# A causal mask that is filled in, rotary queries computed turned, and heads and sample batches in a new order

## The reference

```python
q = (rmsnorm(q_lat, q_norm) @ w_uq).reshape(B, T, H_B, NOPE + ROPE)       # 8 heads, 128 + 64
q = concat([q[..., :NOPE], rope(q[..., NOPE:], pos)])
# rope: x1, x2 = halves of 32; [x1*cos - x2*sin, x2*cos + x1*sin]
s = einsum('bqhd,bshd->bhqs', q, k) * scale
s = where(k_chunk <= q_chunk, s, -inf)    # chunks of 64: masked per 64 x 64 block
o = einsum('bhqs,bshd->bqhd', softmax(s), v) * silu(gate)
x = x + rmsnorm(o @ w_out, norm_post)
```

## Time and profile before

| | us |
|---|---|
| three runs | 620.49, 621.52, 622.27 (median 621.52) |
| the profiled execution | 620.64 |
| its span, first to last instruction | 618.9 |
| TensorE busy | 599.2 (97%) |
| VectorE busy | 369.4 (60%) |
| ScalarE busy | 308.1 (50%) |
| GpSimd busy | 109.8 (18%) |

### The profile page before, as it was taken

How to read it: one execution, slowest core, us unless ns; L and a number is a source line. 1 busy time by engine, 2 the same in 40 slices (tenths; PEclk the granted TensorE clock), 3 DMA queues, 4 the chain that set the end, 5 groups by cost and what they waited for, 6 DMA issues and landing times.

```text
span 618.9 us, 11804 instructions
## 1 busy us (share of the span) xinstructions
PE 599.2 (97%) x4546; PEld 576.6 (93%) x4546; DVE 369.4 (60%) x574; ACT 308.1 (50%) x616; POOL 109.8 (18%) x173
## 2 busy tenths in 40 slices
PE   8999999999999999999999999999999988799996
PEld 7999999999999999999999999989998977699996
DVE  5485667464554872277536478467788875663415
ACT  6796463442362562267326324345656567662311
POOL 0100010010030143156407200110000033400002
PEclk9999999999999999999999999999999999999999
DMA  8932362271262273242425222231110155856004
GB/s 299 348 97 87 101 204 78 73 216 54 78 203 70 79 271 104 61 147 87 135 51 156 69 69 61 60 90 31 35 53 18 51 172 203 252 176 238 1 2 170
DMA packets 65431, 73.46 MB, mean 119 GB/s; under 512 B 8160, under 2 KB 57568, under 8 KB 65248
## 3 DMA queue, kind: packets, MB, share of 16 engines
q1 hardware_dynamic: 65376, 72.71, 36.8%
HBM read 61.92 MB, written 10.78 MB: 117 GB/s over the span
## 4 chain that ended last, share of the span: by engine, by line
PE 70%; DVE 12%; ACT 10%; issue 3%; DMA 3%; POOL 2%; SPq 1%; DVEq 0%; ACTq 0%; POOLq 0%
PE bank L1598 22%; PE bank L1600 21%; PE bank L1599 21%; DVE pT_lo L1297 2%; DMA x_nat<-in_x_sample_dram 2%; ACT prob L1239 2%; DVE sT_lo L1297 1%; ACT slab_hi L1033 1%; DVE slab_lo L1297 1%; PE bank L1874 1%; ACT sT_hi L1033 1%; PE bank L1645 1%; DVE rows L1293 1%; DMA x_raw<-in_xT_dram 1%; ACT qS L1033 1%
## 5 line engine op out<-in xcount | busy, mean ns | idle before, releaser
L1598 PE MATMUL bank<-slab_hi,hat_hi 128*128 128x256 f32 (+2 forms) x560 | 160.4, 286 | 1.8 <-DVE hat_lo L1297 1.0
L1600 PE MATMUL bank<-slab_hi,hat_lo 128*128 128x256 f32 (+2 forms) x560 | 159.3, 285 | 0.0
L1599 PE MATMUL bank<-slab_lo,hat_hi 128*128 128x256 f32 (+2 forms) x560 | 159.3, 285 | 0.0
L1598 PEld LDWEIGHTS bank<-slab_hi,hat_hi 128*128 128x128 f32 x560 | 105.3, 188 | 3.3 <-DVE slab_lo L1297 1.4
L1600 PEld LDWEIGHTS bank<-slab_hi,hat_lo 128*128 128x128 f32 x560 | 105.6, 189 | 0.6
L1599 PEld LDWEIGHTS bank<-slab_lo,hat_hi 128*128 128x128 f32 x560 | 105.2, 188 | 0.6
L1297 DVE TENSOR_TENSOR slab_lo<-stage,slab_hi 128x1024 fp32r<-128x1024 f32 (+3 forms) x70 | 83.7, 1196 | 26.7 <-ACT slab_hi L1033 25.5
L1598 PE MATMUL bank<-hat_hi,slab_hi 128*128 128x320 f32 x256 | 79.4, 310 | 0.7 <-DVE krL L1297 0.4
L1599 PE MATMUL bank<-hat_lo,slab_hi 128*128 128x320 f32 x256 | 78.7, 308 | 0.0
L1600 PE MATMUL bank<-hat_hi,slab_lo 128*128 128x320 f32 x256 | 78.7, 308 | 0.0
L1033 ACT ACTIVATE slab_hi<-stage 128x1024 fp32r<-128x1024 f32 (+3 forms) x70 | 71.0, 1014 | 6.1 <-DMA stage<-in_a_w_in_dram 1.5
(11 more groups left out here) (324 smaller groups left out, 1369.7 us busy)
## 6 DMA issues: line engine op xcount, KB each, us to landing
stage<-in_a_w_in_dram SPq DMA_DIRECT2D x22, 512.0 KB, 4.6
st_s<-in_state_gla_dram SPq DMA_DIRECT2D x4, 1024.0 KB, 6.7
out_dram<-st_s SPq DMA_DIRECT2D x4, 1024.0 KB, 5.1
stage<-in_a_w_out_dram SPq DMA_DIRECT2D x8, 512.0 KB, 4.3
stage<-in_b_w_in_dram SPq DMA_DIRECT2D x8, 512.0 KB, 4.5
stage<-in_ckvT_dram SPq DMA_DIRECT2D x8, 512.0 KB, 4.0
stage<-in_cache_ckv_dram SPq DMA_DIRECT2D x8, 512.0 KB, 6.5
stage<-in_b_w_out_dram SPq DMA_DIRECT2D x8, 512.0 KB, 4.2
```

The source lines that it names most:

```text
L1598: pe.matmul(out, a[0], b[0], start=first, stop=False)
L1599: pe.matmul(out, a[0], b[1], start=False, stop=False)
L1600: return pe.matmul(out, a[1], b[0], start=False, stop=last)
```

## The change

- The mask matmuls and their two constants go. In `S`, VectorE first writes -2^120 with one memset (64 partitions, two pieces of 64 columns) into the scores' bank in PSUM, waits for it, and then takes the maxima.
- The prompt's rotary queries are computed turned: weights (reordered on the host) are stationary, 512 tokens stream. `qr` (g, e) gives half e of four heads, 4 x 32 rows. VectorE rotates with tables laid out alike (`cosT`, `sinT`, loaded by SP in `ldt`); `qh` splits into high and low, and SP sets each head's 32 rows in `qS` with 16 DMAs of 64 KB per group of four heads, 32 in all. The samples' tile keeps the old way (`qo`, `qoT`), ahead of and behind a gate product.
- The rotary weights are loaded with two DMAs, not six.
- Order of heads: the `qabs` of a head comes right behind its scores, the last value tile behind the first head's key, the piece for head h + 4 is multiplied and copied right behind the turn, its low part (`plo`) last in the head; the cached batches are split likewise into `ct` (ScalarE) and `cl` (VectorE) and lie in heads 4 and 5, not 3 and 4.
- Order of sample batches: `ot` and `cr` ahead of `ct`, `cl` behind the scores' maxima, weight pieces at the end of a batch.
- In phase A's tail `xT` of tile 2 is ahead of `rs` of the last tile.

```diff
+        if NT <= t < NT + 3:
+            out += [("xT", "B", t - 3)]
         if t == NT:
             out += [("rs", NT - 1)]
-        if NT <= t < NT + 3:
-            out += [("xT", "B", t - 3)]
         if 0 <= t - 1 < NT - 1:
             out += [("rs", t - 1)]
...
-    out += [("gb", 2, 0), ("cT", 4)] + [("qT", t) for t in range(NT)] + [("gb", 2, 1)]
-    out += [("qr", 0)]
+    out += [("gb", 2, 0), ("cT", 4)] + [("qT", t) for t in range(NT)] + [("ldt",), ("gb", 2, 1)]
+    out += [("qr", 0, 0)]
     load(("gb", 1))
-    out += [("qr", 1), ("qr", 2), ("qrT", 0), ("gb", 1, 0), ("qrT", 1), ("qr", 3), ("qrT", 2), ("qr", 4)]
+    out += [("qr", 0, 1), ("qo",), ("gb", 1, 0), ("qh", 0), ("qoT",), ("qr", 1, 0)]
     load(("gb", 0))
-    out += [("gb", 1, 1), ("qrT", 3)]
+    out += [("qr", 1, 1), ("gb", 1, 1)]
     load(("uvn", 0))
     load(("uvn", 1))
-    out += [("gb", 0, 0), ("qrT", 4), ("gb", 0, 1)]
+    out += [("qh", 1), ("gb", 0, 0), ("gb", 0, 1)]
...
-    out += [("qn", 0), ("kh", 0), ("vh", 1, 2), ("vh", 1, 3), ("qabs", 0)]
-    load(("hd", 3))
+    out += [("qn", 0), ("kh", 0), ("vh", 1, 2)]
...
     for h in range(-1, HB):
         if h >= 0:
             out += [("T", h, 0), ("T", h, 1)]
-        if h == HB - 1:
-            out += [("Oh", h - 1), ("zr", 1), ("ct", 2), ("ss", 1)]
-        else:
-            out += [("S", h + 1, 0), ("S", h + 1, 1), ("N", h + 1, 0), ("N", h + 1, 1)]
+        if 0 <= h < 4:
+            out += [("piece", ("hd", h + 4), 0)]
+        elif 4 <= h < 6:
+            out += [("ct", h - 4)]
+        if h + 1 < HB:
...
-        if h == 6:
-            out += [("cr", 2), ("ot", 2), ("ss", 0)]
-        if h >= 0:
...
-        if h == 0:
-            out[out.index(("T", 0, 1)) + 1:out.index(("T", 0, 1)) + 1] = [("qabs", 1)]
-        if 0 <= h < 4:
...
+        if h == -1:
+            out += [("vh", 1, 3)]
+            load(("hd", 3))
         elif h == 5:
             out += [("zr", 0), ("cr", 0), ("ot", 0), ("cr", 1), ("ot", 1)]
+        elif h == 6:
+            out += [("cr", 2), ("ss", 0)]
+        if 0 <= h < HB - 1:
+            out += [("O", h), ("Oh", h)]
+        if 0 <= h < 4:
+            out += [("plo", ("hd", h + 4), 0)]
+        elif 4 <= h < 6:
+            out += [("cl", h - 4)]
+        elif h == 6:
+            out += [("ot", 2)]
+    out += [("zr", 1), ("ct", 2), ("cl", 2), ("ss", 1)]
...
+        if b == 0:
+            out += [("O", HB - 1)]
         out += [("st", b)] + [("zr", b + 2)] * (b + 2 < SB)
+        if b + 3 < SB:
+            out += [("ot", b + 3), ("cr", b + 3), ("ct", b + 3)]
+        if b + 2 < SB:
+            out += [("ss", b + 2)]
+        if b + 3 < SB:
+            out += [("cl", b + 3)]
+        if b == 0:
+            out += [("Oh", HB - 1)]
+        if b > SB - 3:
+            out += [("y0", b - SB + 2)]
+        if b:
+            out += [("cx", b - 1)]
+        out += [("sv", b), ("cs", b)]
...
-        if b + 3 < SB:
-            out += [("ct", b + 3), ("cr", b + 3), ("ot", b + 3)]
-        if b + 2 < SB:
-            out += [("ss", b + 2)]
-        if b > SB - 3:
-            out += [("y0", b - SB + 2)]
-        if b:
-            out += [("cx", b - 1)]
-        out += [("sv", b), ("cs", b)]
...
+    if step[0] == "qr" and step[2] == 0:
+        return ("pe",)
     if step in APART:
-        return ("sp", "act")
+        return ("sp", "pool", "act") if step[1][0] == "hd" else ("sp", "act")
...
-APART = [("piece", ("qk", 0), j) for j in range(2)]
...
+    return ("plo", *step[1:]) if step in APART else ("cl", step[1]) if step[0] == "ct" else step
...
+                    after(sp, "pe", "qT", NT - 1)
+                    for to, x in ((cosT, "cosT"), (sinT, "sinT")):
+                        sp.dma_start(to[:, :], dram[x]).then_inc(tables_in, 16)
...
+                    after(sp, "dve", "qh", g)
+                    if g == 0:
+                        sp.wait_ge(kept_out, 16 * NT)
+                    for i, x in enumerate((rot_hi, rot_lo)):
+                        for e in range(2):
+                            to = qS[i * ROPE + e * RH:i * ROPE + (e + 1) * RH, :, :]
+                            for h in range(4):
+                                sp.dma_start(raw(to[:, 4 * g + h, :]), raw(x[e][h * RH:(h + 1) * RH, :])).then_inc(rotary_in, 16)
...
+                elif kind == "qh":
+                    g = step[1]
+                    after(act, "dve", "qr", g, 1)
+                    if g:
+                        act.wait_ge(rotary_in, 16 * 16 * g)
+                    for e in range(2):
+                        last = copy(rot_hi[e][:, :], rot[e][:, :])
...
+                    if step[1] == 0:
+                        act.wait_ge(rotary_in, 16 * 32)
...
+                    g = step[1]
+                    if g == 0:
                         dve.wait_ge(latent_out, 16 * 4)
+                        dve.wait_ge(tables_in, 32)
...
+                    x, y = (banks(("qr", g, e))[0][:, 0, :] for e in range(2))
+                    cos, sin, t1, t2 = (v[:, :] for v in (cosT, sinT, *turn))
+                    tt(t1, x, cos, MUL)
+                    link(tt(t2, y, sin, MUL))
+                    link(tt(rot[0][:, :], t1, t2, SUB))
+                    tt(t1, y, cos, MUL)
+                    link(tt(t2, x, sin, MUL))
+                    last = tt(rot[1][:, :], t1, t2, ADD)
+                elif kind == "qh":
+                    for e in range(2):
+                        last = low(rot_lo[e][:, :], rot[e][:, :], rot_hi[e][:, :])
...
-                elif kind == "ct":
+                elif kind == "cl":
                     b = step[1]
-                    last = low(sT_lo[b % NKEYS][:, :, 0:PAST], staged_as("ct", step), sT_hi[b % NKEYS][:, :, 0:PAST])
+                    after(dve, "act", "ct", b)
+                    last = low(sT_lo[b % NKEYS][:, :, 0:PAST], staged_as("ct", ("ct", b)), sT_hi[b % NKEYS][:, :, 0:PAST])
                 elif kind == "S":
                     _, h, u = step
+                    i0, i1 = UNITS[u]
+                    apart = 512 + (i1 - i0) * P
+                    link(dve.memset(row[0:P // 2, i0 * P:i0 * P + 2 * apart].rearrange("p (j n) -> p j n", n=apart)[:, :, P // 2:P], NEG))
...
+                    _, g, e = step
                     ready("uqr")
                     after(pe, "dve", "qT", NT - 1)
+                    w = [x[:, g * PIECE:g * PIECE + KQ * 256].rearrange("p (k n) -> p k n", n=256)[:, :, e * P:(e + 1) * P] for x in weights("uqr")]
+                    for k in range(KQ):
+                        last = mm3(bank[:, 0, :], cut(w, A_, k), cut(qlT, A_, k, slice(0, SEQ)), k == 0, k == KQ - 1)
+                elif kind == "qo":
                     for g in range(2):
                         w = [x[:, g * PIECE:g * PIECE + KQ * 256].rearrange("p (k n) -> p k n", n=256) for x in weights("uqr")]
                         for k in range(KQ):
-                            last = mm3(bank[:, 0, g * 256:(g + 1) * 256], cut(qlT, A_, k, slice(t * P, (t + 1) * P)), cut(w, A_, k), k == 0, k == KQ - 1)
...
+                    pe.wait_ge(rotary_in, 16 * 32)
+                    after(pe, "dve", "qoT")
...
                         pe.matmul(o, qS[:, h, q], krS[:, keys], start=False, stop=False)
-                        pe.matmul(o, qS[:, h, q], krL[:, keys], start=False, stop=False)
-
-                        last = pe.matmul(bank[:, j, q], cst_r("early"), cst_r("late"), start=False, stop=True)
+                        last = pe.matmul(o, qS[:, h, q], krL[:, keys], start=False, stop=True)
...
+                    after(pe, "dve", "cl", b)
                     after(pe, "pool", "ot", b)
+                    after(pe, "pool", "cr", b)
```

More of the change, by code:

```diff
@@ L362 @@
 STAGE_NEXT = {}
-APART = [("piece", ("qk", 0), j) for j in range(2)]
+APART = [("piece", ("qk", 0), j) for j in range(2)] + [("piece", ("hd", h), 0) for h in range(4, HB)]
 def low_step(step):
-    return ("plo", *step[1:]) if step in APART else step
+    return ("plo", *step[1:]) if step in APART else ("cl", step[1]) if step[0] == "ct" else step
 FIRST_WEIGHTS = [STAGED_NO["piece", ("g", 0), j] for j in range(2)]
@@ L596, in program @@
         cn_s = sb("cn_s", [P, KL])
+        qab_at = place[0]
         qab = pair("qab", [P, KC, SB, HB * SL])
@@ L627, in program @@
         place[0] = temp_at
-        qrn, rtmp = [sb(f"qrn{i}", [P, HB * ROPE]) for i in range(2)], sb("rtmp", [P, HB * ROPE])
+        turn = [sb(f"turn{i}", [P, SEQ]) for i in range(2)]
+        place[0] = rows_at
+        cosT, sinT = sb("cosT", [P, SEQ]), sb("sinT", [P, SEQ])
+        place[0] = qab_at
+        rot = [sb(f"rot{e}", [P, SEQ]) for e in range(2)]
+        rot_hi, rot_lo = ([sb(f"rot_{x}{e}", [P, SEQ], fp32r) for e in range(2)] for x in ("hi", "lo"))
+        qrn = sb("qrn", [P, HB * ROPE])
+        assert place[0] <= temp_at
         place[0] = temp_at
@@ L1536, in _ @@
-                    last = rotate(qrn[t % 2][:, :].rearrange("p (h n) -> p h n", n=ROPE), v, tables, rtmp)
```

(14 more changed lines are left out.)

90 lines of the change are left out of this document (45 added, 45 removed), and 2 rows, old and new, of the table PARTS.

## The result

The changed kernel takes 616.21 us (median of 6 runs, 614.85 to 617.79) and the one before 621.89 (6 runs, 620.49 to 624.72): ratio 0.9913, 95% interval 0.9892 to 0.9933. It is 5.7 us faster where 10.3 had been forecast. The profiled execution took 617.37 us; its span is 615.6.

A forecast was written before the change was run, and what follows sets the result against it. TensorE was taken as the bound, with a VectorE-ScalarE loop as long in the heads. Terms -0.9 - 3.5 - 0.9 - 0.4 + 0 - 4.6 = -10.3 us gave 610.3, 611.2 as median; range 607.5 to 616.5.

The forecast's parts named there:

- Tail of phase A: End of phase A: tile 2's copy ahead of the last tile's square closes a TensorE wait, -0.9 us (bounds 0 and -1.03).
- Rotary queries: Before the heads: 32 of 40 transposes go, -3.5 us (bounds -3.2 and -3.6); the transfers in place are hidden.
- that rival: Before the first scores: rotary transfers end last if an issue takes over 0.8 us; at 1.38, 629 us; chance 0.06.
- Masks: Heads' scores: mask matmuls of the first two heads count, -0.9 us; the other six go to VectorE's loop, 0.
- Sample batches: Sample streams: the new order closes TensorE's 5.0 us of waits for GpSimd; -4.6 us after the seam (bounds 0 and -5.0).
- tied to its loads: Sample stage bound by loads or VectorE, leaving 2.5 to 5 of the 4.6, or costlier memsets and waits: 615 us; chance 0.22.
- At the seam with the last head: Between head and sample stages: VectorE, late from its loop, gives back 0.4 us of the 5.0 gained in the streams.
- the first rival: Sample stage tied to its loads or to VectorE, or memset and waits taking as much: 615 us; chance 0.22.

The follow-up runs named there:

- filled: Changed kernel with 40 needless matmuls of 264 columns ahead of the wait of the first stream's scores: 615.82 us, ratio 0.9908 to the kernel before.
- ss_behind_o: Changed kernel with the scores of stream 0 behind O and Oh of head 6 instead of ahead of them: 613.92 us, ratio 0.9888 to the kernel before.
- qabs7_early: Changed kernel with qabs of head 7 alone back in its old place, one head earlier: 609.81 us, ratio 0.9827 to the kernel before.
- old_orders: Changed kernel with the old order of heads and sample streams, keeping turned rotary queries, memset and phase A's tail: 618.10 us, ratio 0.9958 to the kernel before.
- mixed_cl1: Changed kernel with qabs 7 one head earlier, mask matmuls for heads 2 to 7, stream 1's cache split behind N of head 7: 607.97 us, ratio 0.9794.

## Why the prediction was right or wrong

The sign and the bound were right; the size was 5 us too good, and the time lies in the stated range by only 0.3 us. By its own steps, in the prediction's order:

- **Tail of phase A, -0.9.** The wait of 1.03 is gone. One of 0.17 is left:

```profile
293.53 0.36 PE L1661 MATMUL bank<-slab_hi,hat_hi 128*128 128x256 f32 x1 [0.17 <-DVE hat_lo L1335]
```

 It stands one tile later, at the next split, which is not moved. From the first of phase A's last turns (275.92 before, 277.74 after) to the latent's last turns (345.22 and 346.74), 69.30 us became 69.00: -0.3. The other traces with this order have 68.62 to 69.10, the two without it 69.31 and 69.41, so it is worth 0.2 to 0.8. By itself it was not tried.
- **Rotary queries, -3.5.** With the masks still there the way to T 0 fell from 76.72 to 73.28, -3.4 for transposes and order of `qabs`. Right. SP's timeline shows the transfers:

```profile
373.23 5.04 SPq L916 DMA_DIRECT2D qS<-rot_hi  x8
378.31 5.03 SPq L916 DMA_DIRECT2D qS<-rot_lo  x8
...
395.65 5.02 SPq L916 DMA_DIRECT2D qS<-rot_lo  x8
```

 An issue takes 0.63 us, not the 0.33 taken, against the 0.8 from which that rival decides; the last landed by 404 and the first scores started at 410.24. Hidden, but by 6 us and not by 16.

```profile
qS<-rot_hi SPq DMA_DIRECT2D x16, 64.0 KB, 2.1
```

 They land in 2.1 us, where the earlier trace rows had been used for 4.0. The cost was in the issues, as the prediction said. The Trainium skill, "SBUF — State Buffer", section "Door 1: The DMA port swizzle", puts the 1 MB of a group at some 5 us (an estimate from its 218 GB/s); the 16 issues of a group took 10, so this limit was never tested.
- **Masks, -0.9.** The size of a memset was over-rated and its worth too. The group of them:

```profile
L1618 DVE MEMSET bank<- 64x128 f32 x16 | 2.6, 165 | 2.8 <-PE bank L1896 1.5
```

 It runs 0.17 and the next instruction starts 0.20 after it, against 0.31. By the Trainium skill, "VectorE: DVE Perf Modes", section "Zero memsets can be issued as uint32 (trn2)", 128 elements are 0.13 us (an estimate); the reciprocal's 0.17 as a fixed part on top of it was my addition, and the row refutes that. The heads came 11.7 apart where I said 11.9, with 0.37 to 0.51 of wait in each. What failed is the counterfactual: I held the loop at 11.86 whatever the order, less 0.28 for the weight copy. With the masks on TensorE the new order runs at 11.43, so the six masks did not go for nothing; they cost 0.27 a head. Alone the edit is a loss of 1.3 us, in the whole change one of some 2.0.
- **Sample batches, -4.6.** The waits for GpSimd closed, and streams got under my 5.0 to 5.2: 4.87. Alone -5.5, in the whole -6.9 (the first streams no longer carry heads' work): both are past the stated bound of -5.0, which was the sum of the waits alone. The rival "tied to its loads" falls: in this trace no engine waits for a load between st 0 and st 7, and the DMA share is 0.73 in the stream shown above.
- **The step that failed**: "At the seam with the last head VectorE, late from its loop, gives 0.4 back". It gave 8.3 back. I had noted that `qabs` moves one head later, and priced it at -0.4 for VectorE's loop; I did not ask who waits for the last one. The wait was in the code of `ss` all along. Some 5.1 us are the wait and 2.2 to 2.7 the clock behind it, by the trace of filled. Moving `qabs` 7 alone back takes 6.9 us off, and puts the kernel at 609.8, or at 611.1 by its ratio, beside the forecast of 611.2. That nearness is in part luck: against the kernel before that kernel still loses 1.8 us at the seam, and the heads (-1.65) and the streams (-6.8) give more than was forecast. The time of the changed kernel came out where the first rival put it, but not by its mechanism.

## What to carry to other kernels

Where a step is moved later in a loop, follow its last instance into the next stage: the consumer that waits for "all of them" is not in the loop, and the loop's profile does not show it. Work shifted from a full engine to one that is half idle can be a loss if the half-idle one is a link in a chain with waits to both sides; ask how long the chain would be without it, in the new order. Where several edits come together, try each alone: here one was worth as much as all, and one was a loss.

## What the chip showed

- An idle time can cost TensorE more than its length. After 5.09 us of it the granted clock was 0.50 (1.2 GHz) for some 5 us and the matmuls of 264 columns started 0.22 us apart, not 0.12; with needless matmuls in the idle time it stayed at 1.00. In ss_behind_o a wait of 2.92 us was enough. But length alone did not decide. Windows of qabs7_early, the second of two short waits (1.41 us ahead of T 7, then 0.49) and the scores behind it:

```profile
499.57:500.06 0.49, 0.01 (x1) 0.00 (x0) 0.04 (x1) 0.46 (x5) 0.43 (x4) 0.96 1.06 380
500.06:501.00 0.94, 0.94 (x4) 0.94 (x5) 0.00 (x0) 0.91 (x2) 0.18 (x1) 0.50 0.98 279
```

 old_orders has the same two waits at the same place. Its timeline, and the window of the scores behind them:

```profile
500.68 1.28 PE L1894 MATMUL bank<-const,prob 128*128 128x128 f32 x10 [1.40 <-DVE prob L1620]
502.45 0.39 PE L1651 MATMUL bank<-sT_hi,qab_hi 128*128 128x264 f32 x1 [0.48 <-ACT sprob L1295]
```

```profile
502.45:505.37 2.92, 2.20 (x16) 2.02 (x17) 1.72 (x3) 2.83 (x4) 0.17 (x1) 1.00 0.39 136
```

 The first fell to 0.50 and started the next 15 score matmuls 0.22 apart, some 1.5 us lost inside the 7.33 of its T7 to st 0. The second stayed at 1.00, and so did mixed_cl1, whose waits there are longer (1.66 and 1.04). Nor is it sure that the first kernel falls each time: the mean granted clock was 0.996 in the execution traced and 0.998 to 0.999 in its four others. The Trainium skill, "TensorE: Matmul & The Clock Gate", section "HAM oscillation — how this bites in real kernels", describes matmul work cut up by waits for DMA that starts at the lower clock behind each. The changed kernel's wait of 5.09 us agrees; the waits in that example are longer than the two short ones here, and it does not tell what sets qabs7_early and old_orders apart. That stays open.
- VectorE's split of a cache tile, 1.22 to 1.31 us elsewhere in the trace, took 2.21 while GpSimd worked beside it, and GpSimd's small cast next to it 1.08 where its like takes 0.21:

```profile
491.35 1.77 POOL L1024 TENSOR_TENSOR skL<-stage,skS 128x512 fp32r<-128x512 f32 x1
493.19 1.08 POOL L1035 CAST sT_hi<-cT_s_hi 128x32 fp32r<-128x32 f32 x1
```

 By the Trainium skill, "SBUF — State Buffer", section "Who interferes with whom", a VectorE instruction with two inputs in SBUF contends with a GpSimd instruction that reads SBUF; the rows agree. It was not tried by itself.
